# HGRN level products in 14 groups of up to four tiles instead of 21 of two, with VectorE's level scaling issued behind the stream maximum

## What is computed

```
# MLA, each sample stream b, against its 512 cached keys and its 16 own ones
s = q_lat @ ckv.T + q_pe @ kpe.T ; p = softmax(s) ; o = p @ ckv
# HGRN2, within a chunk: causal products with a decay that differs by channel
b = cumsum(logf)
a[t, s] = sum_d q[t, d] * k[s, d] * exp(b[t, d] - b[s, d])      for s <= t
o = a @ i + (q * exp(b)) @ state
```

## Time and profile before

| | |
|---|---|
| median of 3 runs | 2607.15 us (2605.62 to 2608.69) |
| the profiled execution's own time | 2607.52 us |
| its span in the trace | 2605.5 us |
| TensorE busy | 2566.4 us, 99% |
| VectorE, ScalarE, GpSimd busy | 63%, 44%, 20% |
| granted TensorE clock | 0.999 |

### The profile page before, as it was taken

One profiled execution on the slowest core, in us unless ns is written; L12 is line 12 of the kernel. 1 busy time (PEld: TensorE's weight loads), 2 busy tenths in 40 slices (PEclk: granted clock), 3 DMA queues, 4 the chain that ended last, 5 costly groups with the idle time before them and its releaser, 6 DMA issues.

```text
span 2605.5 us, 44639 instructions
## 1 busy us (share of the span) xinstructions
PE 2566.4 (99%) x17912; PEld 2452.4 (94%) x17912; DVE 1640.8 (63%) x2562; ACT 1137.0 (44%) x1920; POOL 531.7 (20%) x440
## 2 busy tenths in 40 slices
PE   9999999999999999999999999999999999999998
PEld 8999999996689999999999999999956899999998
DVE  5666575646466866657577574765564757757473
ACT  5343344424654534334454342553165535434253
POOL 0010112103754101011210110121066441101011
PEclk9999999999999999999999999999999999999999
DMA  3322324220025132232313222334101161322321
GB/s 115 91 81 81 97 66 113 73 59 11 20 54 100 44 87 81 82 97 71 108 33 98 81 71 78 87 89 106 27 11 34 42 130 33 97 81 71 88 83 59
DMA packets 369794, 190.73 MB, mean 73 GB/s; under 512 B 38541, under 2 KB 365536, under 8 KB 369630
## 3 DMA queue, kind: packets, MB, share of 16 engines
q1 hardware_dynamic: 365248, 177.89, 25.5%
q0 software_dynamic: 4000, 10.47, 1.7%
q10 hardware_dynamic: 382, 0.14, 0.0%
HBM read 182.53 MB, written 5.93 MB: 72 GB/s over the span
## 4 chain that ended last, share of the span: by engine, by line
PE 94%; DVE 3%; ACT 1%; issue 1%; DMA 0%; SPq 0%; DVEq 0%; another core or an unknown queue 0%; ACTq 0%
PE ps L727 27%; PE ps L729 27%; PE ps L728 27%; PE ps L1104 2%; PE ps L1115 1%; PE ps L1147 1%; PE ps L1166 1%; PE ps L1156 1%; PE ps L1216 1%; PE ps L1217 1%; DVE at L2688 0%; PE ps L1238 0%; PE ps L1229 0%; PE ps L1328 0%; PE ps L1378 0%
## 5 line engine op out<-in xcount | busy, mean ns | idle before, releaser
L727 PE MATMUL ps<-xh,w 128*128 128x320 f32 x1920 | 595.4, 310 | 3.3 <-DVE css L2950 3.3
L729 PE MATMUL ps<-xh,w 128*128 128x320 f32 x1920 | 593.5, 309 | 0.0
L728 PE MATMUL ps<-xl,w 128*128 128x320 f32 x1920 | 593.4, 309 | 0.0
L1529 ACT ACTIVATE w<-raw 128x512 fp32r<-128x512 f32 (+3 forms) x372 | 315.8, 861 | 486.4 <-PE ps L729 466.2
L3047 POOL TENSOR_TENSOR hl<-ub,hh 128x640 fp32r<-128x640 f32 x88 | 174.1, 1978 | 1448.5 <-ACT hh L1529 1381.3
L727 PE MATMUL ps<-hh,w 128*128 128x320 f32 x1408 | 438.1, 311 | 3.3 <-DVE ub L2344 1.2
L728 PE MATMUL ps<-hl,w 128*128 128x320 f32 x1408 | 435.2, 309 | 0.0
L729 PE MATMUL ps<-hh,w 128*128 128x320 f32 x1408 | 435.2, 309 | 0.0
L727 PEld LDWEIGHTS ps<-xh,w 128*128 128x128 f32 x1920 | 360.4, 188 | 5.5 <-DVE css L2950 3.8
L728 PEld LDWEIGHTS ps<-xl,w 128*128 128x128 f32 x1920 | 360.4, 188 | 0.3
L729 PEld LDWEIGHTS ps<-xh,w 128*128 128x128 f32 x1920 | 360.4, 188 | 0.0
(11 more groups left out here) (415 smaller groups left out, 4674.1 us busy)
## 6 DMA issues: line engine op xcount, KB each, us to landing
raw<-in_w_ffn_in_dram SPq DMA_DIRECT2D x176, 512.0 KB
raw<-in_w_ffn_out_dram SPq DMA_DIRECT2D x192, 192.0 KB
raw<-in_w_in_dram SPq DMA_DIRECT2D x38, 512.0 KB
raw<-in_w_ffn_out_dram SPq DMA_DIRECT2D x64, 128.0 KB
wraw<-in_w_out_dram SPq DMA_DIRECT2D x8, 512.0 KB
raw<-in_w_out_dram SPq DMA_DIRECT2D x8, 512.0 KB
out_dram<-xio SPq DMA_DIRECT2D x5, 512.0 KB
xin<-in_x_prompt_dram SPq DMA_DIRECT2D x4, 512.0 KB, 7.5
```

Of the source, the lines that this page charges most:

```text
L727: pe.matmul(out, wh, xh, start=first, stop=False, skip_group_check=loose)
L728: pe.matmul(out, wh, xl, start=False, stop=False, skip_group_check=loose)
L729: return pe.matmul(out, wl, xh, start=False, stop=last, skip_group_check=loose)
L1529: return nc.scalar.activation(out, in_, func, **kw)
```

## The change

`LEVEL_STEPS` becomes 14 entries: levels 0 to 2 one group of 4 tiles each, levels 3 to 6 a group of 3 tiles and one of 2, level 7 groups of 2, 2 and 1. A table says which groups go into the two places of each turn of the loop: one group in turns 0 and 1 (levels 2 and 3), two in turns 2 to 5, the second group of level 7 alone in the first place of turn 6 and the last alone in the second place of turn 7. Two groups go ahead of the loop. On VectorE `scaled` of level 2 moves ahead of the normalising of stream 1, and `scaled` of level b+3 from the end of turn b to the place behind the maximum of stream b+2.

```diff
-LEVEL_STEPS = [(n, tuple(range(t, min(t + 2, PT_ if n < 3 else TILES))))
-               for n in range(NLEV) for t in range(0, PT_ if n < 3 else TILES, 2)]
-THIRD = (1, 4)
+LEVEL_STEPS = [(n, range(t, min(t + w, PT_ if n < 3 else TILES)))
+               for n, w in enumerate((4, 4, 4, 3, 3, 3, 3, 2)) for t in range(0, PT_ if n < 3 else TILES, w)]
+LEVELS_AT = ((2, None), (3, None), (4, 5), (6, 7), (8, 9), (10, 11), (12, None), (None, 13))
...
             stream_scores(l, 1)
-            level_step(l, 2)
-            m = 3
             for b in range(NSEQ):
+                first, second = LEVELS_AT[b]
                 if b + 2 < NSEQ:
                     stream_keys(l, b + 2)
                     stream_rope_keys(l, b + 2)
-                level_step(l, m)
+                if first is not None:
+                    level_step(l, first)
                 if b + 1 < NSEQ:
                     stream_transpose(l, b + 1)
                 if b + 2 < NSEQ:
                     stream_scores(l, b + 2)
                 if b == NSEQ - 1:
                     stream_values(l, b)
-                level_step(l, m + 1)
+                if second is not None:
+                    level_step(l, second)
                 if b < NSEQ - 1:
                     stream_values(l, b)
-                m += 2
-                if b in THIRD:
-                    level_step(l, m)
-                    m += 1
...
             stream_maximum(1)
-            level(2)
+            scaled(l, 2)
             stream_normalise(1)
-            scaled(l, 2)
-            m = 3
             for b in range(NSEQ):
-                level(m)
+                first, second = LEVELS_AT[b]
+                if first is not None:
+                    level(first)
                 if b + 2 < NSEQ:
                     stream_maximum(b + 2)
+                if b < NLEV - 4:
+                    scaled(l, b + 3)
                 if b == NSEQ - 1:
                     stream_output(b)
-                level(m + 1)
+                if second is not None:
+                    level(second)
                 if b + 2 < NSEQ:
                     stream_normalise(b + 2)
                 if b < NSEQ - 1:
                     stream_output(b)
-                m += 2
-                if b in THIRD:
-                    level(m)
-                    m += 1
-                if b < NLEV - 4:
-                    scaled(l, b + 3)
```

## The result

The change made the kernel slower: 2616.86 us in the median of 6 runs (2616.31 to 2620.58) against 2607.71 us for the kernel before in the same session (2605.62 to 2608.69), a ratio of 1.0037 with a 95% interval of 1.0027 to 1.0047. The forecast was 2609.7 with a range up to 2614.0: the loss was 9.15 us instead of some 2.5. The profiled execution took 2616.31 us, its span is 2614.1 and its granted clock 0.997 (before 2607.52, 2605.5 and 0.999).

What follows compares the result with a forecast made beforehand. TensorE was taken as the bound. The stretch adds 0.77 and ScalarE's delay 0.48, so 1.25 us a layer, 2.5 in two: 2609.7 us, with its own range 2607.3 to 2612.9, widened to 2604.0 to 2614.0.

Steps and rivals of the forecast that it cites:

- Prices of the groups: Level products on TensorE take 1.92 for four tiles, 1.48 for three; VectorE's copies 1.42 and, at levels 5 and 6, 1.88.
- the dearer prices of 1.52 and 1.97: VectorE's copies priced without a shared start, for four tiles and for three of level 5 or 6; gives 2610.2 us.
- The stretches: Eight terms from the first level product to `front(0)`, summing to 61.39 against 60.62 us, +0.77 a layer.
- The waits: TensorE's idle times from the first level product to `front(0)`: 4.32 us a layer, the largest 1.19 before level 2.
- Rival (b): Slower: each new wait on TensorE costs more than charged, 3.8 us in all, 2613.5 us; chance 0.15.
- One term of the end: At level 7, TensorE's second pair waits for the copy and starts 2.61 us after the scores.
- ScalarE's delay: Behind `front(0)`, `darg` starts 1.90 us after it instead of 1.42, so `front(1)` comes 0.48 later a layer.
- The other queues: GpSimd's distances 4 to 6, stream 0's reload (cover 1.8 us) and SyncE's output projection loads hold nothing up; no cost.
- No clock is to be won: Over the whole execution the granted clock is 0.999, so nothing can be gained from it.

Runs made afterwards that it cites:

- experiments 3 and 4: Changed kernel with eight filler matmuls in layer 0's idle time: 2616.63 us; fillers ahead of levels 1 and 2 added: 2614.85; those with GpSimd's product made to wait: 2611.19.
- experiment 5: The change's parts apart: the 14 groups with scalings at their old places, 2631.37 us; the kernel before with only the scalings moved, 2613.46 us.
- last version: Changed kernel with scalings ahead of the maximum, two GpSimd waits, last groups shifted, and stream 0's normalising and transposes put ahead in the prelude: 2606.68 us.
- experiment 3: Changed kernel with eight unread matmuls on TensorE in layer 0, between level 7's second pair and the transposes of stream 7: 2616.63 us.

## Why the prediction was wrong, point by point

- **Prices of the groups: right.** x32 starts its successor after 1.94 (forecast 1.92), three tiles take 1.5; copies of four tiles take 1.43 (1.42), those of three at levels 5 and 6 1.87 and 1.90 (1.88), so the dearer prices of 1.52 and 1.97 did not come.
- **The stretches: right.** Their sum up to stream 7 was 51.30, measured 51.55. The 0.25 are in the first: the copy of level 0 started 2.26 after its group, not 2.13, and level 1 started 0.15 after that copy's end, not 0.05.
- **The waits: right in place and nearly in size.** 0.81, 0.98, 0.38 and, ahead of the values of streams 6 and 7, 0.79 and 0.47, forecast 0.80, 1.19, 0.48, 0.82 and 0.57. The first is partly luck: level 1 started 0.24 later than forecast, but the keys ahead of it took 1.09 instead of 0.88, which also made the wait of 1.19 one of 0.98. Rival (b), each wait dearer by a hand-over, falls as the cause.
- **One term of the end: too small.** The second pair of level 7 was to start 1.25 + 1.31 + 0.05 = 2.61 after the scores. It started at 2.71 in layer 1 and at 3.06 in layer 0 (757.29 - 754.23), since the copy began 1.31 and 1.66 after the products. The wait is 0.24 and 0.58, forecast 0.20. In layer 0 this 0.35 is what brought the normalising beside GpSimd's product.
- **ScalarE's delay: right.** `front(1)` waits 0.42 for `darg` in layer 1, forecast 0.48.
- **The failed step is "The other queues".** It asked of GpSimd only whether its work would be late for others, looked at the distances of levels 4 to 6 and at the reload, and never at the product behind them. It costed at nothing that VectorE's normalising could fall together with that product; the row that told of the near miss in the kernel before (755.11, 0.47 after the normalising's first instruction at 754.64) was not read. The sum's own times would not have shown a meeting either: with 2.61 for the second pair against 3.10 for the product some 0.5 us lie between them, as in layer 1, where 0.37 were left. What was missing is that this margin was thinner than the error of one term, and that losing it costs far more than the term. Taking the meeting away gave 2611.67, inside the forecast's own range; what is left over 2608.12, 3.55 us, stands against the 2.5 forecast and agrees roughly with the trace of that run, where the second `front` comes 1.9 us later in layer 0 and 1.5 in layer 1.
- **"No clock is to be won" hid that one could be lost.** Every wait was priced at its own length. The one of 2.53 cost about 2 us more, as shown in experiments 3 and 4, and in experiment 5 the same held at level 2.
- **What stays open:** why the first copy of level 7 starts 0.35 us later in layer 0 than in layer 1 of the kernel after; and what decides in which executions the clock falls, at the start of the output projection, at the end of the program or elsewhere, in the old kernel too.

## What to carry to other kernels

When a change moves VectorE's work by some microseconds, lay its new times beside GpSimd's instructions, not only beside those that wait for it: look in the old trace for an SBUF-to-SBUF instruction of VectorE that a long GpSimd instruction just misses, and for those released by the semaphore that is moved. A wait on GpSimd that orders the two costs its queue less than a microsecond and here was worth 5 to 18. And price an idle TensorE above its length once it exceeds the waits that the kernel already has: the one of 2.53 here cost some 2 us more.

## What the runs showed of the hardware

- A VectorE instruction of 0.23 us took 2.93 beside a GpSimd instruction of 2.88, 1.59 beside one of 1.54, and 3.40 beside a DMA issue and two instructions of 1.26 in a row, without getting in between. VectorE's scaling, SBUF to SBUF too, was held as well (1.84 instead of 0.82, at 722.17 with scaling first).
- A DMA issue of GpSimd alone did much less in that same trace: the instruction of 0.23 took 0.23 within one issue of 0.75 (747.14) and 0.54 within another (2040.96). Why VectorE did not get in when the issue ahead of the two instructions of 1.26 had ended stays open.
- Copies out of PSUM were not held (1.35 for two tiles beside the product).
- The granted clock came to 0.50 behind TensorE's idle times of 2.53 (kernel after), 2.54 (product in halves; TensorE resumed at 763.85 at 1.00, the clock is 0.66 from 764.5 to 767 and 0.50 from there), 2.66 (groups alone) and 3.45 (scaling first). It also fell behind 1.79 and 1.92 ahead of the output projection, in two profiled executions and not in those with 1.77 (kernel before) and 1.84 (last version), and behind 0.98 in one (experiment 3) and not in others.
